# A sixth expert weight buffer, and expert weights loaded pair by pair

## What is computed

```
scores = sigmoid(x @ w_router)                    # 256 x 64, then group-limited top 8
routed = sum over a token's 8 experts e of gate_e * (silu(x @ w_gate[e]) * (x @ w_up[e])) @ w_down[e]
x      = LN(alpha * x + routed + shared_expert(x))
```

## Time and profile before

| | |
|---|---|
| median of 3 runs | 1317.0 us (1316.55 to 1317.29) |
| span of the profiled execution | 1321.5 us |
| PE busy | 1304.1 us, 99% |
| DVE, ACT, POOL busy | 33%, 20%, 6% |
| HBM read | 448.26 MB, 340 GB/s over the span |

### The profile page before, as it was taken

The page is one execution under the profiler, slowest core; times in us unless marked ns, Lnnn a source line. Parts: engine busy times, 40 slices in busy tenths (PEclk is TensorE's granted clock), DMA queues, the critical chain, the costliest instruction groups (busy, mean ns, idle before and its releaser), DMA issues.

```text
span 1321.5 us, 23482 instructions
## 1 busy us (share of the span) xinstructions
PE 1304.1 (99%) x9812; PEld 759.1 (57%) x9812; DVE 441.5 (33%) x960; ACT 264.9 (20%) x524; POOL 79.9 (6%) x122
## 2 busy tenths in 40 slices
PE   9999999999999999999999999999999999999997
PEld 8889443435534343549688998834444353444533
DVE  2245122222312222227664555522223122222313
ACT  1231211111111111112432330211111111111111
POOL 7302000000000000000002101100000000000001
PEclk9999999999999999999999989999999999999999
DMA  5698799999999999996543006799999999999995
GB/s 178 168 374 326 291 421 420 421 422 422 422 408 422 422 422 422 421 398 186 173 161 98 4 15 265 313 384 418 423 421 422 423 415 413 422 422 423 421 421 212
DMA packets 98823, 450.38 MB, mean 341 GB/s; under 512 B 16192, under 2 KB 45504, under 8 KB 49088
## 3 DMA queue, kind: packets, MB, share of 16 engines
q1 hardware_dynamic: 98752, 449.34, 84.8%
HBM read 448.26 MB, written 1.05 MB: 340 GB/s over the span
## 4 chain that ended last, share of the span: by engine, by line
PE 96%; DVE 3%; ACT 1%; issue 0%; POOL 0%; DVEq 0%; POOLq 0%
PE PS L1950 31%; PE PS L1992 17%; PE PS L2000 10%; PE PS L1921 7%; PE PS L536 4%; PE PS L498 3%; PE PS L1412 2%; PE PS L1437 2%; PE PS L1398 2%; PE PS L1964 2%; PE PS L1972 1%; PE PS L1575 1%; PE PS L1591 1%; PE PS L521 1%; PE PS L2007 1%; PE PS L2079 1%
## 5 line engine op out<-in xcount | busy, mean ns | idle before, releaser
L2310 DVE TENSOR_TENSOR y_parts<-PS,y_parts 128x512 fp32r<-128x512 f32 x128 | 88.5, 692 | 216.5 <-ACT y_parts L2212 216.5
L2284 DVE SCALAR_TENSOR_TENSOR AR<-AR,PS 128x256 f32<-128x256 f32 x64 | 30.7, 480 | 381.3 <-ACT AR L2190 381.3
L2000 PE MATMUL PS<-y_parts,token_map 128*128 128x512 f32 x496 | 143.1, 415 | 0.0
L2000 PEld LDWEIGHTS PS<-y_parts,token_map 128*128 128x128 f32 x496 | 84.6, 188 | 61.3 <-issue 49.5
L1992 PE MATMUL PS<-AR 128*64 128x512 f32 x512 | 116.9, 598 | 0.0
L1992 PE MATMUL PS<-RING,AR 128*64 128x512 f32 x384 | 116.8, 598 | 0.0
L2212 ACT CAST y_parts<-PS 128x512 fp32r<-128x512 f32 x128 | 75.0, 586 | 171.9 <-PE PS L1992 171.9
L1950 PE MATMUL PS<-RING,xT 128*64 128x512 f32 x480 | 108.2, 592 | 1.2 <-issue 1.2
L1950 PE MATMUL PS<-AR,xT 128*64 128x512 f32 x480 | 108.1, 592 | 0.2 <-issue 0.2
L1950 PE MATMUL PS<-RING,AR 128*64 128x512 f32 x480 | 108.1, 592 | 0.0
L1950 PE MATMUL PS<-AR 128*64 128x512 f32 x480 | 108.1, 592 | 0.0
(11 more groups left out here) (329 smaller groups left out, 1567.1 us busy)
## 6 DMA issues: line engine op xcount, KB each, us to landing
RING<-in_moe_w_gate SPq DMA_DIRECT2D x64, 1024.0 KB, 11.4
RING<-in_moe_w_up SPq DMA_DIRECT2D x64, 1024.0 KB, 13.5
AR<-in_moe_w_gate SPq DMA_DIRECT2D x64, 1024.0 KB, 12.6
AR<-in_moe_w_up SPq DMA_DIRECT2D x64, 1024.0 KB, 14.6
AR<-in_moe_w_down SPq DMA_DIRECT2D x64, 1024.0 KB, 13.3
RING<-in_moe_w_down SPq DMA_DIRECT2D x48, 1024.0 KB, 14.2
GB<-in_moe_w_down SPq DMA_DIRECT2D x16, 1024.0 KB, 14.9
AR<-in_ab_w_in SPq DMA_DIRECT2D x16, 512.0 KB, 4.6
```

What stands on the lines that cost most here:

```text
L2000: ins = nc.tensor.matmul(PS[:, 2 * t + h, :], OHT[:, half, t, :], YS[:, n, h * 512:(h + 1) * 512], start=False, stop=True, skip_group_chec ...
L2284: nc.vector.scalar_tensor_tensor(out=HH[0:2 * B, :].rearrange("p (k j) -> p k j", k=FT), in0=by_row(SIL[0:2 * B, :]), scalar=GC[:, buf:buf ...
L2310: nc.vector.tensor_tensor(YS[:, 1, h * 512:(h + 1) * 512], PS[:, 5 + h, :], YS[:, 0, h * 512:(h + 1) * 512], ALU.subtract).then_inc(q["low ...
```

## The change

Slots within an octet are now (0, 1), (2, 3), (EX, EY) and (2, 3): only slots 2 and 3 are used twice. Loads are issued for whole pairs. Expert 5's gate and up weights are loaded during the mixer before (`prefetch_sixth`), its down weights once `X` is free. To stay within the number of semaphores, two are merged with others. TensorE's order of work is the same.

```
-        AFL = 25300
+        AFL = 25296
+        GUY = nc.alloc_sbuf_tensor_at("GUY", [P, 4096], F32, offset=AR_BASE + 4 * AFL)
...
+            if s == EY:
+                return (GUY[:, 0:2048].rearrange("p (k f) -> p k f", k=KT),
+                        GUY[:, 2048:4096].rearrange("p (k f) -> p k f", k=KT),
+                        X[:, :, :])
...
                 sp.dma_start(WOUT[c].rearrange("p (k c) -> p k c", k=KT),
                              w_out[:, :, c * CB:(c + 1) * CB]).then_inc(s_wo[c], 16)
+            moe[0]["prefetch_sixth"](sp)
             for c in range(2):
                 sp.wait_ge(s_pj, 2 * (8 + c) - 2)
                 load_chunk(sp, w_out, c, 2 + c)
...
                 sp.dma_start(g2b[32 * j:32 * j + 32, :], a["rw_g2"][0][P:160, :]).then_inc(s_lg, 16)
+            moe[1]["prefetch_sixth"](sp)
             for c in range(4):
                 sp.wait_ge(s_pj, TK + 2 * c + 2)
                 load_rw(sp, w_rec, c)
...
+            def prefetch_sixth(sp):
+                g, u, d = wslot(EY)
+                if l:
+                    sp.wait_ge(q["gate_up_done"], PAIRS - 1)
+                sp.dma_start(g, gate_src(wg, 5)).then_inc(q["gu_w"][EY], 16)
+                sp.dma_start(u, gate_src(wu, 5)).then_inc(q["gu_w"][EY], 16)
...
                 sp.dma_start(u, gate_src(wu, 4)).then_inc(q["gu_w"][EX], 16)
+                sp.wait_ge(q["x_split"], 2 + past["x_split"])
+                sp.wait_ge(s_pre, 4 * (l + 1))
+                load_down(sp, 5, EY)
+
+                def load_pair(after, first, slots):
+                    sp.wait_ge(q["gate_up_done"], after + 1 + past["gate_up_done"])
+                    for h in range(2):
+                        load_gate_up(sp, first + h, slots[h])
+                    sp.wait_ge(q["down"], 2 * (after + 1) + past["down"])
+                    for h in range(2):
+                        load_down(sp, first + h, slots[h])
...
-                for e, s in ((5, 1), (8, 0)):
-                    sp.dma_start(wslot(s)[0], gate_src(wg, e)).then_inc(q["gu_w"][s], 16)
+                for h in range(2):
+                    sp.dma_start(wslot(h)[0], gate_src(wg, 8 + h)).then_inc(q["gu_w"][h], 16)
...
+                load_pair(1, 6, (2, 3))
+                load_pair(2, 12, (EX, EY))
+                load_pair(3, 10, (2, 3))
+                with sp.Fori(1, 3) as i:
+                    load_pair(4 * i, 8 * i + 8, (0, 1))
+                    load_pair(4 * i + 1, 8 * i + 6, (2, 3))
+                    load_pair(4 * i + 2, 8 * i + 12, (EX, EY))
+                    load_pair(4 * i + 3, 8 * i + 10, (2, 3))
+                load_pair(13, 30, (2, 3))
+                with sp.Fori(4, OCTS - 1) as i:
+                    load_pair(4 * i - 4, 8 * i, (0, 1))
+                    load_pair(4 * i - 1, 8 * i + 2, (2, 3))
+                    load_pair(4 * i - 2, 8 * i + 4, (EX, EY))
+                    load_pair(4 * i + 1, 8 * i + 6, (2, 3))
+                load_pair(PAIRS - 8, E - 8, (0, 1))
+                load_pair(PAIRS - 5, E - 6, (2, 3))
+                load_pair(PAIRS - 6, E - 4, (EX, EY))
...
-                i = 3
-                load_gate_ups(4 * i + 2, [(8 * i + 5, 1), (8 * i + 8, 0)])
-                load_downs(4 * i + 2, [(8 * i + 5, 1)])
-                load_gate_ups(4 * i + 3, [(8 * i + 6, 2), (8 * i + 7, 3)])
-                load_downs(4 * i + 3, [(8 * i + 6, 2), (8 * i + 7, 3), (8 * i + 8, 0)])
-                load_experts(4 * i + 4, [(8 * i + 9, 1)])
-                load_experts(4 * i + 5, [(8 * i + 10, 2), (8 * i + 11, 3)])
...
                 if spare:
-                    slots = (EX, 1)
+                    slots = (EX, EY)
...
-    nc = _bacc.Bacc("TRN2", target_bir_lowering=False, num_devices=1)
+    nc = _bacc.Bacc("TRN2", target_bir_lowering=False, num_devices=1, dynamic_dma_scratch_size=64)
```

More of the change, by code:

```diff
@@ L36 @@
 EX = 4
+EY = 5
 H0 = 8
@@ L1771, in program @@
         moe_shared = {n: sem("moe_" + n) for n in per_layer} | {
-            "gu_w": [sem(f"gate_up_loaded{s}") for s in range(EX + 1)],
-            "dn_w": [sem(f"down_loaded{s}") for s in range(EX + 1)]}
-        uses = [OCTS, E // 4, E // 4, E // 4, OCTS]
+            "gu_w": [sem(f"gate_up_loaded{s}") for s in range(EY + 1)],
+            "dn_w": [sem(f"down_loaded{s}") for s in range(EY + 1)]}
+        uses = [OCTS, OCTS, E // 4, E // 4, OCTS, OCTS]
         gate_ups = [32 * n - (16 if s in (2, 3) else 0) for s, n in enumerate(uses)]
-        once_an_octet = (0, EX)
+        once_an_octet = (0, 1, EX, EY)
         per_layer |= {"map_copied": PAIRS, "gates_ready": PAIRS, "turned": PAIRS + 1}
@@ L1789, in gate_and_up @@
             def gate_and_up(slot):
+                if slot == EY:
+                    return GUY[:, :].rearrange("p (m k f) -> p k m f", m=2, k=KT)
                 w = flat[:, 0:4096] if slot == EX else RING[:, slot + 1, :] if slot < 2 else odd[:, slot - 2, :]
@@ new lines, in loads @@
+                sp.wait_ge(q["first_gates"], 1 + past["first_gates"])
+                for h in range(2):
+                    sp.dma_start(wslot(h)[0], gate_src(wg, 8 + h)).then_inc(q["gu_w"][h], 16)
+                sp.wait_ge(q["gate_up_done"], 1 + past["gate_up_done"])
+                for h in range(2):
+                    sp.dma_start(wslot(h)[1], gate_src(wu, 8 + h)).then_inc(q["gu_w"][h], 16)
+                sp.wait_ge(q["down"], 2 + past["down"])
+                for h in range(2):
+                    load_down(sp, 8 + h, h)
@@ new lines, in loads @@
+                load_pair(PAIRS - 8, E - 8, (0, 1))
+                load_pair(PAIRS - 5, E - 6, (2, 3))
+                load_pair(PAIRS - 6, E - 4, (EX, EY))
+                sp.wait_ge(q["gate_up_done"], PAIRS - 2 + past["gate_up_done"])
+                for e, s in ((E - 2, 2), (E - 1, 3)):
+                    sp.dma_start(wslot(s)[0], gate_src(wg, e)).then_inc(q["gu_w"][s], 16)
+                for e, s in ((E - 2, 2), (E - 1, 3)):
+                    sp.dma_start(wslot(s)[1], gate_src(wu, e)).then_inc(q["shared_and_last_ups_loaded"], 16)
@@ L1888, in loads @@
+                sp.wait_ge(q["down"], 2 * (PAIRS - 2) + past["down"])
+                for e, s in ((E - 2, 2), (E - 1, 3)):
+                    load_down(sp, e, s)
                 if l == 0:
@@ L2023, in pe_pair @@
                 a_pass = [1 if s in once_an_octet else 2 for s in slots]
-                use = [int(p >= 2) if s != EX else 0 for s in slots]
+                use = [int(p == 3) for s in slots]
                 for s, n, u in zip(slots, a_pass, use):
@@ L2497, in gp_moe @@
                 nc.gpsimd.memset(pads(XGD), 0.0).then_inc(q["pads_cleared"], 1)
-            return dict(load_expert=load_expert, prefetch=prefetch, loads=loads, pe=pe_moe, gp=gp_moe, act=act_moe, dve=dve_moe)
+            return dict(load_expert=load_expert, prefetch=prefetch, prefetch_sixth=prefetch_sixth, loads=loads, pe=pe_moe, gp=gp_moe, act=act_moe, dve=dve_moe)
         moe = [moe_view(l) for l in range(2)]
```

28 lines of the change are left out of this document (7 added, 21 removed).

## The result

The changed kernel takes **1320.8 us** in the median of ten runs (1319.6 to 1323.5). The kernel before, run beside it, takes 1317.95 (1315.8 to 1320.0). The ratio is 1.0023, with an interval of 1.0014 to 1.0032: slower by 1.8 to 4.2 us. The forecast was 1320.9.

What follows compares the result with a forecast made beforehand. TensorE, busy 1304.1 of 1321.5 us, was taken to bound the kernel, with DMA just under it. A 3.3 us stall at chunk 2 plus 0.6 us at pair 30 took 1317.0 to 1320.9 us, range 1316.6 to 1322.8.

Steps and rivals of the forecast that it cites:

- What can be won: Expert loops, both layers: TensorE's waits for expert weights total 1.4 us, all that the sixth buffer can win.
- The loads ahead of chunk 2: Layer 0's mixer: two 1 MiB loads ahead of the half chunks delay chunk 2 by 5.0 us; TensorE stalls 3.3 us.
- short-tail rival: Rival at chunk 2: its late landing is accidental or absorbs part of the loads; stall 0.1 to 2 us; chance 0.25.
- The cooled clock: Rival: the stall at chunk 2 halves TensorE's clock, costing another 1.7 to 3.4 us; chance 0.10.
- stall term: TensorE's forecast wait before chunk 2 in layer 0's mixer: 3.3 us, range 0.1 to 3.3.
- The dry queue: Before pair 15's loads, SP waits for pair 13's product; the DMA queue idles about 5 us and the lead is lost.
- The wait at pair 30: Late in each layer's expert loop: wait of 0.9 us instead of 0.6; both layers +0.6 us (-1.2 to +0.6).
- Layer 1's early loads: Layer 1's mixer: expert 5's two early loads fit into a gap between SP's issues at 601.7 and 620.2; cost nothing.
- expert 5's down load: Now ahead of SP's wait for `first_gates`; delays only gate loads of experts 8 and 9, wanted 50 us later; nothing.
- the merged semaphores: They count in the same order as before and wait for nothing new; cost nothing.
- The sum: Whole kernel: 3.3 us stall plus 0.6 us for expert waits, 1317.0 + 3.9 = 1320.9 us, 0.3% slower.
- The rival without a stall: Rival: chunk 2 overtakes the early loads and pair 30's stalls vanish; 1315.8 us, counted as no change; chance 0.12.

Runs made afterwards that it cites:

- The kernel without any wait for expert weights: Changed kernel, layer 0's early loads behind the half chunks, gate/up loads of experts 32, 33, 36 and 37 issued sooner: 1319.16 us, ratio 0.9993 to the kernel before.
- the first experiment: Changed kernel with expert 5's gate and up loads in layer 0 behind the four half chunks: 1319.48 us, ratio 1.0003; run again, 1320.24 us, 1.0005.

## Why the prediction was right, point by point

- **What can be won.** Right. The kernel without any wait for expert weights is 0.6 us below the one before in the median, within the error.
- **The loads ahead of chunk 2.** The mechanism was right, and it is the whole of the measurable loss: it appears with the two loads alone and goes when they are moved. The price was nearly right too: 2 x 2.485 = 5.0 us predicted, 4.5 measured from SyncE's first issue at this place (14.1 and 18.6 us), 4.7 in the mean of the profiles. The size of the wait was off: 3.3 us predicted, 2.3 measured (2.2 to 3.9 over the four profiles with 2 MiB ahead and nothing in the wait). What failed is that SyncE's and TensorE's times were taken over from one execution. In the new profile SyncE came to the place 0.8 us earlier, which shortened the wait, and TensorE 0.3 us earlier, which lengthened it. Only 0.5 us was absorbed by the tail of the queue, less than the short-tail rival had it. The issue of chunk 2's second half landed after 14.0 us and not the 16 that I named.
- **The cooled clock.** This was a rival with a chance of 0.10, and it came true in all five profiles that have a wait of 2.2 us or more there, at 1.70 to 1.76 us each. The weighing failed: I had no idle stretch of that length in the trace and took the 0.63 us at pair 30 as evidence against it. Waits of 2.20 and 2.30 us, shorter than the one I forecast, were followed by it. The Trainium skill, TensorE: Matmul & The Clock Gate (Part 1: The HAM clock gate), has idle stretches bring the array to 1.2 GHz. The granted clock of 0.53 behind a wait of 2.30 us agrees.
- **So the forecast's number is right in part by luck.** Its stall term, 3.3, stands against 2.3 + 1.76 = 4.06 in the profile: a wait taken too long stood in for a clock that was left out. And 1320.9 meets 1320.8 only because the kernel before took 1317.95 beside it and not the 1317.0 that I started from. The step between the two kernels, +3.9 us forecast and +2.85 measured, was 1 us too large.
- **The dry queue.** Right: no bytes from 327 to 332.7, 364 GB/s over the octet, first landing after 4.7 us. SyncE's wait for pair 13 gives the lead back, and the experiment with the new order in octet 3 gets part of it.
- **The wait at pair 30.** Predicted 0.9 us in each layer, +0.6 in all against before; measured none in layer 0 and 0.51 in layer 1, with 0.27 at pair 27: 0.8 in all against 1.4, so -0.6. The failed step is the value picked from the bounds. The last load landed at 569.97, 93 loads of 2.50 us after 337.4; I had taken 2.504. That and TensorE's later arrival of a few tenths turn 0.9 into nothing. The term can't be had from one execution anyway. The three profiles of the changed kernel have 0.8, 1.1 and 2.2 us of waits for expert weights, a mean of 1.4, which is what the kernel before had. The old order varies as well: the kernel before with the two loads added has 0.4.

```profile
PE PS L1954 <- issue: 1.1, 3, 0.4
```

```profile
PE PS L1954 <- issue: 2.2, 3, 1.1
```

  (The table of waits of the second and of the third profile of the changed kernel.) So for the expert loops no profile shows a gain or a loss beyond this variation.
- **Layer 1's early loads, expert 5's down load, the merged semaphores.** Costed at nothing, and no profile has a wait that they caused. The kernel with the early loads of layer 0 late and all of these in place is at 1.0003 and 1.0005.
- **The sum.** +3.9 us forecast. Profiled: 2.3 + 1.76 - 0.6 = 3.5, less 0.3 for TensorE's earlier arrival. Median: +2.85. The short-tail rival (0.25) gave 0.1 to 2 us of wait; the three profiles of the changed kernel have 2.3, 2.5 and 3.9. The rival without a stall (0.12) fell with chunk 2's landing at 83.14.

What stays open: how often the half clock follows the wait in the timed runs, and with it how the median's 2.85 us is shared between the two; and why the kernel with one load ahead loses 2.2 us in the median with a profiled wait of 0.64.

## What to carry to other kernels

A load that is issued "while there is room" is not free where the queue is deep: price it by its bytes at the queue's rate (here 2.4 us for each MiB) against the slack of the first urgent load behind it, and put it behind that one. Take the slack from several executions, since the issuing engine can be late by more than the slack itself (here 2.5 us between the earliest and the latest). A buffer gives lead only as far as the issuing engine's order lets it; look for the wait in that order at which the queue runs dry, and count what the lead can win at all before building it (here 1.4 us). When the stall that is forecast on TensorE is as long as those that had a half clock behind them here (1.85 us and more), add a term for it, and compare stretches, not spans, where the clock varies between executions.

## What the runs showed of the hardware that I had not expected

- **A short idle time is enough to bring TensorE's clock down.** After waits of 1.85, 2.20, 2.25, 2.30, 2.49 and 3.85 us the clock was at 1.2 GHz for 3.4 us, beginning up to 1.4 us after work had started again. After 0.64 us (one load ahead) and 0.83 us (a wait for expert weights in the first experiment), and where small products filled the wait, it stayed at 2.4 GHz. So a wait of 2.3 us costs 4.1 in the trace. With waits of 3.44, 4.36 and 10.2 us it fell during the wait and stayed down for 5.5, 5.5 and 3.3 us behind it.
- **The half clock among the RWKV products comes and goes.** It was there twice, once or not at all in executions of kernels that are equal in that stretch, for 0 to 10.2 us in all, and the stretch lasts 77.8 to 83.5 us. That is more than the whole effect of this change. The timed runs have the same spread: of the kernel before, on the three chips of the experiments, the 16 executions with a mean clock of 0.999 took 1318.1 us on average, the 23 with 0.996 took 1320.7.
- **What a queue's loads cost the next one is nearly linear in their bytes**, once it is counted from the issuing engine's own arrival: 3.0 us for one MiB, 4.7 for two, 12.4 for five. Counted from the start of the kernel the same two MiB seemed to cost 3.6 us, because SyncE's arrival differs between executions.
